# A two-layer decoder trunk with 64 experts: shared down products moved into the expert loop, routing reordered, last scatter and sums by column halves

## What is computed

```python
aff = jax.nn.sigmoid((xt @ w_router).astype(jnp.float32))
sel = aff + router_bias
# 4 of 8 groups by the sum of their top 2, then the top 8 experts of these
gates = jnp.take_along_axis(aff, eidx, axis=-1)
gates = gates / jnp.sum(gates, axis=-1, keepdims=True) * ROUTED_SCALE
h = jax.nn.silu(xb @ w_gate[e]) * (xb @ w_up[e])     # xb: the rows of expert e
routed = segment_sum((h @ w_down[e]) * gate)
shared = (jax.nn.silu(xt @ ws_gate) * (xt @ ws_up)) @ ws_down
return routed + shared                               # then x <- LN(alpha*x + moe)
```

## Time and profile before

| | us |
|---|---|
| Median of 3 runs (lowest to highest) | 1285.56 (1285.19 to 1286.29) |
| The profiled execution | 1285.14 |
| its span, first to last instruction | 1282.9 |
| TensorE busy (matmuls) | 1215.6, 95% |
| VectorE busy | 366.9, 29% |
| ScalarE busy | 293.0, 23% |
| GpSimd busy | 49.8, 4% |
| DMA | 446.60 MB, 348 GB/s on the mean |

### The profile page before, as it was taken

The page is one execution under the profiler, slowest core; times in us unless marked ns, Lnnn a source line. Parts: engine busy times, 40 slices in busy tenths (PEclk is TensorE's granted clock), DMA queues, the critical chain, the costliest instruction groups (busy, mean ns, idle before and its releaser), DMA issues.

```text
span 1282.9 us, 20916 instructions
## 1 busy us (share of the span) xinstructions
PE 1215.6 (95%) x7984; PEld 768.6 (60%) x7986; DVE 366.9 (29%) x913; ACT 293.0 (23%) x703; POOL 49.8 (4%) x97
## 2 busy tenths in 40 slices
PE   7999999999999999999899989999999999999994
PEld 6775756565565656565677647565656655565652
DVE  0334712221222222221424447222212222222214
ACT  1453312121221212121123313121212212121211
POOL 1331000000000000000012100000000000000000
PEclk9999999999999999999999989999999999999998
DMA  9532499999999999999930525999999999999993
GB/s 345 189 138 122 202 398 421 420 421 423 422 421 422 422 422 421 422 422 421 406 129 1 202 90 214 399 420 421 421 421 421 422 422 421 422 422 422 422 420 130
DMA packets 70800, 446.60 MB, mean 348 GB/s; under 512 B 6880, under 2 KB 10336, under 8 KB 20576
## 3 DMA queue, kind: packets, MB, share of 16 engines
q1 hardware_dynamic: 69744, 442.79, 83.9%
q10 hardware_dynamic: 1008, 3.15, 0.6%
HBM read 444.86 MB, written 1.05 MB: 348 GB/s over the span
## 4 chain that ended last, share of the span: by engine, by line
issue 49%; PE 36%; DMA 10%; DVE 1%; POOL 1%; ACT 1%; SPq 0%; another core or an unknown queue 0%; POOLq 0%; DVEq 0%; ACTq 0%
DMA ring<-in_w_up 10%; PE bank L953 7%; PE bank L978 6%; PE bank L946 6%; PE bank L524 4%; PE bank L987 3%; PE bank L582 3%; PE bank L543 2%; POOL soft L501 1%; PE bank L846 1%; DMA ring<-in_w_in_a 1%; PE bank L960 1%; PE bank L758 1%; PE bank L864 1%; PE bank L558 1%
## 5 line engine op out<-in xcount | busy, mean ns | idle before, releaser
L953 PE MATMUL bank<-ring,work 128*64 128x256 f32 x2048 | 232.9, 380 | 21.3 <-DMA ring<-in_w_up 21.3
L978 PE MATMUL bank<-ring,work 128*64 128x512 f32 x1024 | 233.8, 598 | 4.3 <-ACT work L1057 4.3
L946 PE MATMUL bank<-ring,work 128*64 128x256 f32 x2048 | 232.4, 379 | 2.3 <-DMA ring<-in_w_gate 1.3
L946 PEld LDWEIGHTS bank<-ring,work 128*64 128x64 f32 x2048 | 150.9, 137 | 100.4 <-issue 39.8
L953 PEld LDWEIGHTS bank<-ring,work 128*64 128x64 f32 x2048 | 154.4, 137 | 91.9 <-issue 29.0
L1554 DVE TENSOR_TENSOR yhalf<-bank,yhalf 128x512 fp32r<-128x512 f32 x128 | 88.6, 692 | 239.4 <-ACT yhalf L1057 239.4
L987 PE MATMUL bank<-yhalf,back 128*128 128x512 f32 x512 | 150.8, 417 | 2.8 <-DVE yhalf L1554 2.8
L978 PEld LDWEIGHTS bank<-ring,work 128*64 128x64 f32 x1024 | 68.1, 136 | 134.3 <-issue 128.4
L1546 DVE SCALAR_TENSOR_TENSOR work<-work,gcol,bank 128x256 f32<-128x256 f32 x64 | 30.8, 481 | 370.2 <-issue 289.7
L1057 ACT ACTIVATE yhalf<-bank 128x512 fp32r<-128x512 f32 x128 | 76.5, 598 | 220.5 <-PE bank L978 220.5
L987 PEld LDWEIGHTS bank<-yhalf,back 128*128 128x128 f32 x512 | 87.3, 190 | 39.7 <-issue 23.8
(11 more groups left out here) (149 smaller groups left out, 754.5 us busy)
## 6 DMA issues: line engine op xcount, KB each, us to landing
ring<-in_w_gate SPq DMA_DIRECT2D x128, 1024.0 KB, 19.5
ring<-in_w_up SPq DMA_DIRECT2D x128, 1024.0 KB, 21.2
ring<-in_w_down SPq DMA_DIRECT2D x128, 1024.0 KB, 18.9
ring<-in_w_in_b SPq DMA_DIRECT2D x3, 3072.0 KB, 23.4
ring<-in_w_out SPq DMA_DIRECT2D x4, 2048.0 KB, 8.2
ring<-in_w_mem_kv SPq DMA_DIRECT2D x2, 2048.0 KB, 18.6
ring<-in_w_in_a SPq DMA_DIRECT2D x1, 3072.0 KB, 17.4
ring<-in_w_shared_gate SPq DMA_DIRECT2D x2, 1024.0 KB, 6.0
```

Of the source, the lines that this page charges most:

```text
L946: last = pe.matmul(gate_bank[slots_of(e), 0:HID], xg[:, k, slots_of(2 * j + e)], w[e][:, k, 0, :], start=(k == 0), stop=(k == KT - 1))
L953: last = pe.matmul(up_bank[slots_of(e), 0:HID], xg[:, k, slots_of(2 * j + e)], w[e][:, k, 1, :], start=(k == 0), stop=(k == KT - 1))
L978: last = pe.matmul(yb[half][slots_of(e), :], hT[:, f, slots_of(e)], w[e][:, f, half * 512:half * 512 + 512], start=(f == 0), stop=(f == FT ...
```

## The change

- Routing: VectorE makes the ranks and the first one-hots directly after `chosen` and the shared hidden rows of tile 0; the number of rounds and the gates come after. The ranks now count from 1 (`iota0` starts at 1), so a copy and a subtraction fall away. `slot_no` is copied before the logits. TensorE makes the rank products after two steps of the last shared part, and the other six steps behind them.
- `x_low(1)` runs on GpSimd.
- The shared expert's down weights no longer lie in the ring slot but in `acc`, loaded once attention no longer uses it. The slot is free after the shared gate and up products.
- `shared_turn` of both tiles is made in unit 0 of the first round, and the four down quarters in units 0, 1, 28 and 29. The other three `sums` are opened by the scatter.
- The first round stands alone on TensorE and ScalarE; the number of rounds is read after it, and more rounds stand in an `If`. VectorE keeps its loop and makes the next round's first one-hots at the end of each round, also of the last.
- The last scatter goes by column halves, each sum closed at once; the last norm of tile 1 and its store go by halves.

```diff
-        hsT = work[:, 0:512].rearrange("p (f n) -> p f n", f=FT)
+        hsT = work[:, 7680:8192].rearrange("p (f n) -> p f n", f=FT)
...
+        shared_wd = acc[:]
...
             if it[1] == "shared":
-                sp.wait_ge(sem(f"shared_down_{it[0]}"), 2 * TT)
+                sp.wait_ge(sem(f"shared_gu_{it[0]}"), TT)
...
+                for n, k in enumerate(first_experts[l]):
+                    if n == 1:
+                        sp.wait_ge(sem("softened"), sum(len(jobs[i]) for i in range(l + 1)))
+                        sp.dma_start(shared_wd, by_row_pair(ws_down[l])).then_inc(sem(f"shared_wd_landed_{l}"), 16)
...
+                t = TT - 1
+                pool.wait_ge(sem("xhi"), TT * l + t + 1)
+                pool.tensor_tensor(by_chunk(xhalf[:, 1, t, :]), by_column(x[:, t, :]), by_chunk(xhalf[:, 0, t, :].bitcast(F32)),
+                                   ALU.subtract).then_inc(sem("xlo"), 1)
...
                 shared_part(1, 0)
-                shared_part(1, 1, range(KT - 2))
-                shared_turn(0)
-                shared_part(1, 1, range(KT - 2, KT)).then_inc(sem(f"shared_gu_{l}"), 1)
+                shared_part(1, 1, range(2))
...
-                shared_down(0, 0)
-                shared_turn(1)
-                shared_down(0, 1)
-                for half in range(2):
-                    shared_down(1, half)
-                pe.wait_ge(sem(f"routed_{l}"), 1)
-                rounds = pe.value_load(nround_i[0:1, l:l + 1], min_val=0, max_val=3) + 1
-
+                shared_part(1, 1, range(2, KT)).then_inc(sem(f"shared_gu_{l}"), 1)
...
+                    if shared == 0:
+                        shared_turn(0)
                     turn_h(U)
+                    if shared == 0:
+                        shared_turn(1)
                     if not first:
-                        scatter(U - 1, (j - 1) % OCT_PAIRS, (2, 3))
+                        scatter(U - 1, (j - 1) % OCT_PAIRS, (2, 3), starts)
+                    if shared is not None:
+                        shared_down(shared)
...
-                    scatter(r * PAIRS + PAIRS - 1, OCT_PAIRS - 1)
-                for n in range(4):
-                    pe.matmul(sums[n][:], zeros[:, 0:P], zeros[:], start=False, stop=True).then_inc(s_("summed"), 1)
+                one_round(0, True)
+                pe.wait_ge(sem(f"routed_{l}"), 1)
+                extra = pe.snap(pe.value_load(nround_i[0:1, l:l + 1], min_val=0, max_val=3))
+                with pe.If(extra > 0):
+                    with pe.Fori(1, extra + 1) as r:
+                        scatter(r * PAIRS - 1, OCT_PAIRS - 1)
+                        one_round(r)
+                for half in range(2):
+                    pe.wait_ge(s_("y_parted"), extra * (2 * PAIRS) + (2 * PAIRS - 1 + half))
+                    for t in range(TT):
+                        scatter_quarter(2 * t + half, OCT_PAIRS - 1)
+                        pe.matmul(sums[2 * t + half][:], zeros[:, 0:P], zeros[:], start=False, stop=True).then_inc(s_("summed"), 1)
...
                 dve.wait_ge(sem("chosen"), l + 1)
                 shared_hidden(0)
+                g = G[l, "rank"]
+                filled(dve, g)
+                link(dve.scalar_tensor_tensor(out=rank[:], in0=bank_of(g, TT, NE), scalar=1.0, in1=chosen[:], op0=ALU.add, op1=ALU.mult))
+                one_hot8(0, 0, 0)
+                one_hot(0, 0, 0, 0)
+
+                dve.tensor_reduce(cmax[:], bank_at(g)[:, TT * NE:2 * TT * NE], AX_X, ALU.max).then_inc(read, 1)
...
-                x_low(1)
...
                     dve.tensor_scalar(slot_no[:], slot_no[:], float(TILE_SLOTS), None, ALU.add).then_inc(s_("slots_set"), 1)
+                    one_hot8(r * OCTETS + OCTETS, 0, r + 1)
+                    one_hot(r * PAIRS + PAIRS, 0, 0, r + 1)
                 for n in range(4):
                     t, half = n // 2, n % 2
-                    dve.wait_ge(s_("summed"), n + 1)
+                    dve.wait_ge(s_("summed"), 2 * half + t + 1)
```

More of the change, by code:

```diff
@@ L980, in down, with scatter_quarter, scatter, unit @@
                         last.then_inc(s_("down_done"), 1)
-                def scatter(U, b, quarters=range(4)):
+                def scatter_quarter(q, b, start=False):
+                    t, half = q // 2, q % 2
+                    for n in range(2):
+                        pe.matmul(sums[q][:], back[b][:, t, :], yhalf[:, n, half * 512:half * 512 + 512],
+                                  start=start and n == 0, stop=False)
+                def scatter(U, b, quarters=range(4), starts=()):
                     pe.wait_ge(s_("y_parted"), 2 * U + 2)
                     for q in quarters:
-                        t, half = q // 2, q % 2
-                        for n in range(2):
-                            pe.matmul(sums[q][:], back[b][:, t, :], yhalf[:, n, half * 512:half * 512 + 512],
-                                      start=False, stop=False)
-                def unit(r, o, j, first=False, last=False):
+                        scatter_quarter(q, b, q in starts)
+                def unit(r, o, j, first=False, last=False, shared=None):
                     O = r * OCTETS + o
@@ L1008, in _, with one_round @@
                 pe.wait_ge(sem("xlo"), TT * (l + 1))
-                with pe.Fori(0, rounds) as r:
+                def one_round(r, shared=False):
                     gather(r * OCTETS, None)
                     pe.wait_ge(s_("xg_dve"), r * 4 * OCTETS + 5)
+                    if shared:
+                        pe.wait_ge(s_("gates_set"), 1)
                     turn_back(r * PAIRS, 0, 0)
                     for j in range(OCT_PAIRS):
-                        unit(r, 0, j, first=(j == 0))
+                        unit(r, 0, j, first=(j == 0), shared=j if shared and j < 2 else None)
                     with pe.Fori(1, OCTETS - 1) as o:
@@ L1244, in _ @@
                     for j in range(OCT_PAIRS):
-                        unit(r, 0, j)
+                        unit(r, 0, j, shared=shared and j == 0)
                     with act.Fori(1, OCTETS - 1) as o:
```

130 lines of the change are left out of this document (72 added, 58 removed).

## The result

The changed kernel takes 1278.99 us in the median (1278.07 to 1279.61, 4 runs), the kernel before 1285.38 us (1285.13 to 1286.29, 4 runs) beside it: a ratio of 0.995, 95% interval 0.9938 to 0.9962. A second set of runs gave 1278.58 against 1285.22 us, ratio 0.9943 (0.9930 to 0.9957). It is faster by 6.4 us, a little over half of the forecast gain of 11.5 us. That lies inside the stated range (1271.2 to 1281.6), but outside the 1271.2 to 1277 that the prediction gave to its forecast: it is the part that was kept for rivals 1 and 2. The profiled execution took 1278.07 us with a span of 1276.0 us, 6.9 us less than before.

The account below looks back on a forecast made before the run. The weight stream was taken to pace the expert loop, so its earlier start counts in full: -11.2 - 1.1 - 0.4 + 0.8 + 0.4 = -11.5 us, giving 1274.1 us; stated range 1271.2 to 1281.6, forecast's own 1271.2 to 1277.

Parts of the forecast that it names:

- rivals 1 and 2: First: GpSimd blocks VectorE during x_low(1), 1281.3 us, chance 0.25; second: TensorE's jump must fetch code, 1279.0 us, chance 0.12.
- Rival 4: Expert loop: TensorE sets the pace after all, so moved work costs 13.4 us more; 1287.5 us, chance 0.04.
- (a): Routing to first gate product in each layer: reordered queues start it 5.6 us earlier, 11.2 us in sum.
- (b): Routing: x_low(1) on GpSimd takes 4.5 us, ends before the gather needs it and doesn't slow VectorE; cost none.
- (c): Shared turns and down products in the expert loop: 0.4 us of standstill in all plus 0.8 us in the last octet.
- just in time: Unit 0: first down reload, 8.7 us behind the gate reload, comes 1.3 us later; gate and up reloads feed 10.0 us.
- (d): End of the kernel: last sums start 1.1 us earlier, limited by VectorE's unneeded one-hots; output by halves saves 0.4 us.
- rival 2: TensorE's jump past unused rounds fetches code: 4.2 us in layer 0, 0.7 at the end; 1279.0 us, chance 0.12.
- Layer 0's end: Scatter ends 1.2 us earlier without gain, since TensorE later waits for in_w_in_b; 2.3 us of jump delay are free.

Follow-up runs that it names:

- the probe: Changed kernel with six pairs put ahead: a long GpSimd pass, one short VectorE instruction inside; beside GpSimd's scaling a VectorE product took 0.77 us; no kernel time given.
- no_down: Changed kernel with the shared down quarters all placed in octet 4, their sixteen matmuls then left out; 1757.7 us, with a second round in layer 1.
- no_if: Changed kernel without the bodies of the further rounds on TensorE and ScalarE, register loads kept; 1278.53 us, ratio 0.9955 to the kernel before.
- gsc_reduce: Changed kernel with VectorE's group scores made by a one-input reduction in place of the sum of two operands; 1281.5 us, one run.
- xlow_vector: Changed kernel with x_low(1) back on VectorE behind the first one-hots; 1280.06 us, ratio 0.9955 to the kernel before.

## Why the prediction came out as it did

The sign and the main mechanism held: the loop is bound by the stream, and what starts the stream earlier counts for most of its size (4.43 us at the first reload of layer 0, 3.97 at the last up product; 6.78 and 5.20 in layer 1). The number lies in the stated range only because that range made room for rivals 1 and 2; the forecast's own part of it, 1271.2 to 1277, was missed. Rival 4 (TensorE paces) is out for the loop as a whole: the up products still wait. It is true in small of the last octet, where the moved products used up the waits. Point by point:

**(a) Start of each loop.** The step from `chosen` on was right and a little cautious: 9.99 and 9.76 us to the gate product, predicted 10.6, before 16.26 (158.99 - 142.73). (The sum's own terms, 153.2 + 0.1 against 158.99, give 5.7 and not 5.6.) That the first VectorE evacuation is next in line was right, too; the register load ahead of it, taken as 0.4, cost 0.24 us in layer 1 (the evacuation at 793.82, the work before it to 793.58) and at most 0.49 in layer 0.

**(b) x_low(1) on GpSimd, "cost: none".** This is the step that failed. The duration was mis-sized on the safe side: 2.85 us where I took 4.5. But what I had reduced to a rival with a chance of 0.25 happened, at its short end: priced at 1.9 us, measured 1.84 and 1.92. I had weighed against the Trainium skill, SBUF — State Buffer, "Who interferes with whom", and let the row win. By that rule VectorE is held until GpSimd is through, and the trace of this case agrees for the two-input pass (2.03 us and 2.11 us for instructions of 0.19). For GpSimd's one-input scaling, which reads SBUF as well, the probe disagrees: it lets VectorE through after about 1.1 of its 2.85 us. So the row misled because it showed another form of GpSimd pass. I had named the width of VectorE's operand as the possible catch; it was the wrong difference.

With it came something not in the sum: TensorE was idle for 1.91 us, and its clock was at 1.2 GHz for the next 3 us in layer 0. That cost 1.45 us of product time (4.26 against 2.81), mostly covered, since the gather had to wait for VectorE anyway: the gains of the two layers differ by only 0.2 us.

**(c) Shared products in the loop, 1.2 us.** Measured 2.0 in the pair of traces, with half a us of scatter from run to run. The terms were placed wrongly. Up to the wait ahead of the last octet the loops grew by 1.20 and 0.93 us (387.05 and 386.86 before), where 0.2 each was priced; in the last octet layer 1 lost 0.65 (59.65 before), priced at 0.8, and layer 0 gained 0.74 (60.60 before, with the wait of 1.09 us for in_w_gate that is now gone), priced at nothing. That the down reload would go out 10.0 us behind the gate reload was right (9.99), that it is "just in time" was not: the stream fell to 371 GB/s for 4 us; no loss in the loop can be tied to that. The quarters' place explains some 0.3 us a layer, in the last octet. The 1.1 us ahead of it are there with the quarters in the middle and, in the one loop of no_down, with no down product at all (388.19). There the wait that ends 252.4 us behind the first reload is where it was before (252.9 and 252.6), and the next one ends at 268.6 instead of 267.8 and 267.5. Where that comes from stays open.

**(d) The end.** -1.20 against -1.1, and -0.5 against -0.4. The one-hots for a round that doesn't come were the limit, as worked out, and the jump was hidden behind them: rival 2 had left 0.7 for it here, and it cost nothing.

**Layer 0's end, "no gain there and 2.3 us free".** The second failed step. The sum put TensorE's jump there at nothing; it made a hole of 3.53 us, about half of the 6.5 us that rival 2 supposed, and the next stage lost 1.84 us instead of its 4.2. The clock fell there too, behind 3.5 us of idleness, which made the scatter 1.3 us a quarter instead of 0.7. I had not counted that the early end of a layer can be lost by other means than the stream. With the hole away (no_if) 1.8 us come back at the next stage and 3.2 don't, 2.94 of them in the wait for in_w_in_b.

So it was not one rival that came but two at once, each at or below its lower price, and part of the loss was made up by chance: the steps from `chosen` on were 0.6 and 0.9 us a layer better than priced. I had given them chances as if they excluded each other. A case with both, at what they measured, would have stood at -11.5 + 3.8 + 1.8 = -5.9 us, 1279.7 against the 1279.0 measured.

## What to carry to other kernels

When a stream paces the loop, read each wait ahead of it down to the one queue that releases it, and then sort that queue by what is needed first: moving work off VectorE brought nothing of its own here, putting the four evacuations ahead of the gates, and the first `turn_back` behind the gate product, brought 2.0 to 2.2 us a layer. A row that speaks against a known conflict must show the same forms on both engines; if it doesn't, price the conflict in full. A branch over unused code cost TensorE both its hole and, beside the stream, a slow clock behind it; moved into the loop, where TensorE had waits to lose, it cost 1.2 and 1.4 us there and gained nothing on the whole. Rivals that can happen together need a case of their own.

## What the runs showed of the hardware

- VectorE's wait for GpSimd shows inside the duration of its own instruction (0.19 us became 2.03), not as idle time. It hits two-input products, and also a one-input scaling from SBUF to SBUF (2.11 us), but not a reduction (0.29 us).
- GpSimd's two-input pass over 128x1024 elements took 2.34 us with plain operands and 2.85 us in the order that the kernel needs; one-input scalings took 2.85 us and held VectorE for only some 0.6 us.
- TensorE's jump past unused code left it idle for 3.4 to 3.6 us at the end of layer 0 (400 GB/s moved by the DMA engines meanwhile), for 4.3 and 4.5 us inside the loop (419 and 421 GB/s), and for 0.5 to 1.0 us at the end of layer 1 with the DMA engines idle (0 GB/s). That fits a fetch that queues behind the stream; it was not shown by itself. (The Trainium skill, Runtime: NRT & Kernel Launch, "Instruction fetch mechanics", says that a taken jump whose target has not been prefetched must fetch it before going on; the traces agree with that rule, and they give it a price.)
- The granted clock fell to 1.2 GHz in some places behind waits of 1.9, 2.7, 3.5 and 4.5 us and stayed at 2.4 GHz behind others of 1.9 us (layer 1 of the changed kernel), so a wait of 2 us can cost 1.5 us more or nothing. Where it fell over the gather and the gate product (gsc_reduce, 5.65 us instead of 3.67; xlow_vector, 5.23) nothing covered it.
